# Delta-rule recurrence as two chains with banks and waits of their own, and the modulation chunks dealt out anew

## What is computed

```python
def gated_delta_chunk_scan(q, k, v, beta, log_a, s0):
    # a_mat = I + strict lower part of beta * (k k^T) * decay; w, u = a_mat^-1 applied to scaled k and v
    def step(state, inp):
        v_new = u_c - w_c @ state
        o = qd_c @ state + qk_c @ v_new
        state = gt_c * state + kd_c.T @ v_new
        return state, o

def run_bidirectional(...):      # one scan forward in time, one backward; their outputs are summed
    oc_f, sc_f = scan_fn(*ctx_fwd, s0);  ox_f, _ = scan_fn(*lat_fwd, sc_f)
    oc_b, sc_b = scan_fn(*flip(ctx_bwd), s0);  ox_b, _ = scan_fn(*flip(lat_bwd), sc_b)

sh1, sc1, g1, sh2, sc2, g2 = split(silu(c) @ w_mod + b_mod, 6)      # and the same for ada_w_2[0], ada_w_2[1]
```

## Time and profile before

| What | us |
|---|---|
| median of 3 runs | 3077.0 |
| lowest and highest | 3072.32, 3078.3 |
| the profiled execution, its own time | 3088.53 |
| its span, first to last instruction | 3086.6 |
| delta rule, half 0: first part, systems and transposes of the inverses, units of the inverses, recurrence, outputs | 396 to 493, 493 to 550, 550 to 646.9, 646.9 to 687.9, 687.9 to 702.6 |
| delta rule, half 1: systems, transposes of the inverses, units of the inverses, recurrence, outputs | 702.7 to 736.1, 736.1 to 751.1, 751.1 to 855.6, 855.6 to 922.9, 922.9 to 934.8 |

### The profile page before, as it was taken

The page is one execution under the profiler, slowest core; times in us unless marked ns, Lnnn a source line. Parts: engine busy times, 40 slices in busy tenths (PEclk is TensorE's granted clock), DMA queues, the critical chain, the costliest instruction groups (busy, mean ns, idle before and its releaser), DMA issues.

```text
span 3086.6 us, 36191 instructions
## 1 busy us (share of the span) xinstructions
PE 2854.6 (92%) x14765; PEld 2144.3 (69%) x14765; DVE 1205.1 (39%) x2187; ACT 579.2 (19%) x1109; POOL 432.9 (14%) x507
## 2 busy tenths in 40 slices
PE   6999978987978599999999989899999999999998
PEld 4677646975944378788878758578874486688843
DVE  2173642873425211111132485366750102576601
ACT  2102012121201211111132255122110111211200
POOL 2152403525411100000000000000110000000100
PEclk8999978998989699999999999899999999999999
DMA  9211340024271599899982200032222221322220
GB/s 368 75 41 42 110 176 27 3 110 164 83 286 43 192 339 333 322 333 331 323 286 83 69 1 1 1 98 93 82 76 75 92 68 41 99 86 82 89 75 27
DMA packets 202849, 403.15 MB, mean 131 GB/s; under 512 B 12850, under 2 KB 100450, under 8 KB 193506
## 3 DMA queue, kind: packets, MB, share of 16 engines
q1 hardware_dynamic: 195522, 375.15, 34.7%
q10 hardware_dynamic: 4896, 17.83, 1.4%
q0 software_dynamic: 2304, 8.39, 0.7%
HBM read 369.88 MB, written 31.46 MB: 130 GB/s over the span
## 4 chain that ended last, share of the span: by engine, by line
PE 84%; DVE 6%; DMA 3%; ACT 3%; issue 2%; POOL 1%; ACTq 0%; SPq 0%; POOLq 0%; DVEq 0%
PE ps L2704 17%; PE ps L1891 11%; PE ps L694 7%; PE ps L1909 5%; PE ps L1617 5%; PE ps L2718 5%; PE ps L2320 4%; PE ps L2733 4%; PE ps L2891 4%; PE ps L686 3%; PE ps L764 2%; PE ps L2462 2%; PE ps L385 2%; PE ps L2494 2%; DMA ring<-in_w_mod 2%
## 5 line engine op out<-in xcount | busy, mean ns | idle before, releaser
L1891 PEld LDWEIGHTS ps<-arena,ring 128*128 128x128 f32 x2944 | 334.2, 193 | 13.3 <-issue 10.5
L1891 PE MATMUL ps<-arena,ring 128*128 128x128 f32 x2944 | 334.5, 276 | 2.4 <-DMA ring<-in_w_gate 2.4
L2704 PE MATMUL ps<-arena 128*128 128x256 f32 x1056 | 235.3, 379 | 1.6 <-DVE arena L2801 1.6
L2704 PEld LDWEIGHTS ps<-arena 128*128 128x128 f32 x1056 | 200.5, 190 | 29.6 <-DVE arena L2801 2.4
L1617 PE MATMUL ps<-ring,hT 128*128 128x512 f32 x384 | 172.7, 606 | 4.2 <-DVE arena L2947 2.6
L694 PE MATMUL ps<-hT,ring 128*128 128x512 f32 x384 | 171.5, 601 | 2.5 <-ACT bet L1034 1.8
L2704 PE MATMUL ps<-hT,ring 128*128 128x256 f32 x704 | 164.9, 389 | 3.3 <-ACTq L200 3.3
L1909 PE MATMUL ps<-ring,arena 128*128 128x512 f32 x368 | 164.0, 598 | 1.8
L2704 PEld LDWEIGHTS ps<-hT,ring 128*128 128x128 f32 x704 | 137.5, 196 | 23.8 <-ACTq L200 4.1
L2718 PE MATMUL ps<-ring,arena 128*128 128x512 f32 x352 | 151.5, 592 | 1.3 <-issue 1.3
L2733 PE MATMUL ps<-ring,arena 128*128 128x512 f32 x352 | 151.7, 592 | 0.0
(11 more groups left out here) (480 smaller groups left out, 4535.8 us busy)
## 6 DMA issues: line engine op xcount, KB each, us to landing
ring<-in_ada_w SPq DMA_DIRECT2D x48, 1024.0 KB, 6.3
ring<-in_w_gate SPq DMA_DIRECT2D x46, 1024.0 KB, 6.6
ring<-in_w_up SPq DMA_DIRECT2D x46, 1024.0 KB, 5.7
ring<-in_w_down SPq DMA_DIRECT2D x46, 1024.0 KB, 5.4
ring<-in_ffn_w_up SPq DMA_DIRECT2D x44, 1024.0 KB, 5.0
ring<-in_w_mod SPq DMA_DIRECT2D x24, 1024.0 KB, 7.8
ring<-in_ffn_w_down SPq DMA_DIRECT2D x20, 1024.0 KB, 4.9
ring<-in_w_in SPq DMA_DIRECT2D x18, 1024.0 KB, 7.8
```

Source lines behind the costliest of these rows:

```text
L1891: last = pe.matmul(ps[:, t, f * P:(f + 1) * P], w[:, k, f * P:(f + 1) * P], xg[:, 4 * c + k, :], start=(c == 0 and k == 0 and f == 0), sto ...
L2704: last = pe.matmul(ps[:, u % 8, 0:HTOK], a[:, k, :], b[:, k, :], start=(k == 0), stop=(k == KD // 2 - 1))
```

## The change

The recurrence handles each direction d by itself. `ks`, `u` and `add` write banks `KSB`, `UB` and `AB`, two per kind, one a direction, and every hand-over (`ks_ps`, `z_ready`, `u_ps`, `u_ready`, `add_ps`, `dS_ready`) counts twice as fast, one step a direction, which `per_side` counts. The matmuls and DVE operations are the same in number and size, but for the dU of a direction, which was an instruction of its own already, and the first state copy, which is cut in two.

The chunks are dealt out anew. First part of half 0: 8 in one row before, now 4 ahead of the 32 transposes and 4 behind them. Systems: 0 and 12 before (halves 0 and 1), now 2 and 6. Inverses: 0 and 8, now 14 and 14, after every second unit from 8 to 34. Recurrence: 8 and 20, now 4 and 8. The last sums of the inverses come at their end. Since a group in bank 6 is now open during the systems of half 0, the projection units there all use bank 7 (`dn_bank`) and wait for the unit before to be copied. The token transposes of half 1 move to k = 2 and 3, four each, and DVE's normalisation steps start at k = 4 rather than 3. ACT's and SP's queues follow the same order; SP loads two chunks between the k and the v weights. POOL's group work is put at other points. The diff of ACT and SP, which repeats this, is left out.

```diff
-                if u >= 2:
+                if name == "dnp" and base and u >= QZ + 2:
+                    pe.wait_ge(s[name + "_out"], base + u)
+                elif u >= 2:
                     pe.wait_ge(s[name + "_out"], base + u - 1)
-                pe_unit(pe, W, name, units, u, 6 + u % 2)
+                pe_unit(pe, W, name, units, u, dn_bank(base and 1, u) if name == "dnp" else 6 + u % 2)
...
-        DN_MODS = [KD, [0] * NC, [0] * NC * LEVELS, [(0, 2), (2, 0), (0, 0), (0, 0), (1, 1), (1, 1)]], \
-            [0, [2] * NC, [int(u in range(10, 42, 4)) for u in range(NC * LEVELS)], [(0, 0)] + [(2, 2)] * 5]
-        DN_TOK = [(0, 0), (0, 2), (2, 1), (1, 2), (0, 0), (0, 0)]
+        def dn_bank(p, u):
+            return TURN_BANK if p and u >= QZ + 2 else 6 + u % 2
+
+        DN_FIRST = [4, 4]
+        DN_MODS = [[0, 2, 0, 0, 0, 0], [int(u in range(8, 36, 2)) for u in range(NC * LEVELS)], [(0, 0), (1, 0), (1, 0), (1, 0), (1, 0), (0, 0)]], \
+            [[1] * NC, [int(u in range(8, 36, 2)) for u in range(NC * LEVELS)], [(0, 0)] + [(1, 1)] * 3 + [(1, 0), (1, 0)]]
+        DN_TOK = [(0, 0), (0, 0), (2, 2), (2, 2), (0, 0), (0, 0)]
...
-            pe_mods(pe, W, DN_MODS[0][0], True)
+            pe_mods(pe, W, DN_FIRST[0], False)
             W.pay()
             pe.wait_ge(s["conv_done"], 1)
...
             last.then_inc(s["tok_ps"], 1)
+            pe_mods(pe, W, DN_FIRST[1], True)
             pe.wait_ge(s["mod_raw"], mods["pe"]["summed"])
             pe_units_between(pe, W, "dnp", DN_UNITS, DU, QZ, QZ + 2)
...
             if i == 0:
                 pe.wait_ge(s["conv_done"], 2)
+                pe.wait_ge(s["mod_raw"], mods["pe"]["summed"])
...
-                pe_mods(pe, W, DN_MODS[p][2][u], False)
+                pe_mods(pe, W, DN_MODS[p][1][u], u == NC * LEVELS - 1)
 
             pe.wait_ge(s["inv_out"], U0 + NC * LEVELS)
             toks, chans = iter(range(8)), iter(range(5))
             for k in range(NC):
                 if k:
-                    pe.wait_ge(s["dS_ready"], (NC - 1) * p + k)
                     for d in range(2):
+                        pe.wait_ge(s["dS_ready"], per_side(NC - 1, p, k - 1, d))
+                        c = ORDER[d][k]
+                        for h in range(2):
+                            last = pe.matmul(ps[:, KSB[d], h * P:(h + 1) * P], KT[:, c, h, :], dS[:, k - 1, 2 * d + h, :], start=True, stop=True)
+                        last.then_inc(s["ks_ps"], 1)
+                    pe_mods(pe, W, DN_MODS[p][2][k][0], False)
...
+                for d in range(2):
+                    if k:
+                        pe.wait_ge(s["z_ready"], per_side(NC - 1, p, k - 1, d))
+                    c = ORDER[d][k]
+                    for h in range(2):
+                        a = 2 * d + h
+                        last = pe.matmul(ps[:, UB[d], h * P:(h + 1) * P], XT[:, c, a, :], tv[:, c, h, :] if k == 0 else zb[:, a, :],
+                                         start=True, stop=True)
+                    last.then_inc(s["u_ps"], 1)
+                pe_mods(pe, W, DN_MODS[p][2][k][1], k == NC - 1 and p == 1)
+                if p == 0:
+                    for _ in range(DN_TOK[k][1]):
+                        pe_tok_group(pe, next(toks))
+                for d in range(2):
+                    pe.wait_ge(s["u_ready"], per_side(NC, p, k, d))
+                    if k < NC - 1:
+                        pe.wait_ge(s["kx_ready"], (NC - 1) * p + k + 1)
...
                         c = ORDER[d][k]
                         for h in range(2):
                             a = 2 * d + h
-                            last = pe.matmul(ps[:, 0, a * P:(a + 1) * P], KT[:, c, h, :], dS[:, k - 1, a, :], start=True, stop=True)
...
+        KSB, UB, AB = [0, 3], [1, 4], [2, 5]
+
+        def per_side(steps, p, k, d):
+
+            return 2 * (steps * p + k) + d + 1
...
-            if p:
-                pool_mods(g, ch, 6)
+            pool_mods(g, ch, 7 if p else 4)
...
-                    g.wait_ge(s["add_ps"], (NC - 1) * p + k - 1)
+                    g.wait_ge(s["add_ps"], 2 * ((NC - 1) * p + k - 1))
...
-                    v.wait_ge(s["ks_ps"], (NC - 1) * p + k)
                     for d in range(2):
+                        v.wait_ge(s["ks_ps"], per_side(NC - 1, p, k - 1, d))
                         c = ORDER[d][k]
                         for h in range(2):
-                            a = 2 * d + h
-                            last = v.scalar_tensor_tensor(out=zb[:, a, :], in0=ps[:, 0, a * P:(a + 1) * P],
+                            last = v.scalar_tensor_tensor(out=zb[:, 2 * d + h, :], in0=ps[:, KSB[d], h * P:(h + 1) * P],
                                                           scalar=nex[:, c, 4 * d + hs + h:4 * d + hs + h + 1],
                                                           in1=tv[:, c, h, :], op0=ALU.mult, op1=ALU.add)
-                    last.then_inc(s["z_ready"], 1)
-                    if p == 0 and k >= 3:
+                        last.then_inc(s["z_ready"], 1)
+                    if p == 0 and k >= 4:
                         next(norm, None)
...
-                v.wait_ge(s["u_ps"], NC * p + k + 1)
                 for d in range(2):
+                    v.wait_ge(s["u_ps"], per_side(NC, p, k, d))
                     c = ORDER[d][k]
-                    last = v.tensor_tensor(dU[:, c, 2 * d:2 * d + 2, :], ps[:, 1, 2 * d * P:2 * (d + 1) * P].rearrange("p (h x) -> p h x", h=2),
-                                           bc(bet[:, c, 4 * d + hs:4 * d + hs + 2], [P, 2, P], 2), ALU.mult)
-                last.then_inc(s["u_ready"], 1)
-                if p == 0 and k >= 3:
+                    v.tensor_tensor(dU[:, c, 2 * d:2 * d + 2, :], ps[:, UB[d], 0:2 * P].rearrange("p (h x) -> p h x", h=2),
+                                    bc(bet[:, c, 4 * d + hs:4 * d + hs + 2], [P, 2, P], 2), ALU.mult).then_inc(s["u_ready"], 1)
+                if p == 0 and k >= 4:
                     next(norm, None)
                 if k < NC - 1:
-                    v.wait_ge(s["add_ps"], (NC - 1) * p + k + 1)
-                    if k == 0:
-                        last = v.tensor_copy(dS[:, 0].rearrange("p a x -> p (a x)"), ps[:, 2, :])
-                    else:
-                        for d in range(2):
-                            c = ORDER[d][k]
+                    for d in range(2):
+                        v.wait_ge(s["add_ps"], per_side(NC - 1, p, k, d))
+                        c = ORDER[d][k]
+                        if k == 0:
+                            last = v.tensor_copy(dS[:, 0, 2 * d:2 * d + 2].rearrange("p a x -> p (a x)"), ps[:, AB[d], 0:2 * P])
+                        else:
+                            v.wait_ge(s["dS_ready"], per_side(NC - 1, p, k - 1, d))
                             for h in range(2):
                                 a = 2 * d + h
                                 last = v.scalar_tensor_tensor(out=dS[:, k, a, :], in0=dS[:, k - 1, a, :],
                                                               scalar=dex[:, 2, c, 4 * d + hs + h:4 * d + hs + h + 1],
-                                                              in1=ps[:, 2, a * P:(a + 1) * P], op0=ALU.mult, op1=ALU.add)
-                    last.then_inc(s["dS_ready"], 1)
-                    v.wait_ge(s["dS_ready"], (NC - 1) * p + k + 1)
-                    if p == 0 and k >= 3:
+                                                              in1=ps[:, AB[d], h * P:(h + 1) * P], op0=ALU.mult, op1=ALU.add)
+                        last.then_inc(s["dS_ready"], 1)
+                    if p == 0 and k >= 4:
                         next(norm, None)
```

55 lines of the change are left out of this document (18 added, 37 removed).

## The result

| | before | after |
|---|---|---|
| median, us | 3076.45 | 3041.58 |
| shortest and longest run, us | 3072.32 and 3078.30 (4 runs) | 3036.99 and 3047.55 (4 runs) |
| ratio to before, with its 95% interval | | 0.989, 0.9868 to 0.9911 |
| the profiled execution and its span, us | 3088.5, 3086.6 | 3047.55, 3045.7 |

What follows compares the result with a forecast made beforehand. PE was taken as the bound (84% of the chain), with gaps in a PE-DVE chain and chunks bunched faster than they load; -10 + 2 + 16 - 5 - 9 + 7.5 - 39 - 2.5 = -40 us gave 3037 us, range 3022 to 3059.

Steps and rivals of the forecast that it cites:

- part 3: Inverses of half 0: 14 chunks at 1.19 us plus sums, less 2 us for DVE's share: +16 us.
- part 6: Inverses of half 1: 6 more chunks at 1.19 us, and the last sums: +7.5 us.
- Part 1: First part of half 0: transposes fill the wait for chunks 5 to 8, k units start sooner: -10 us.
- cold k units: Rival: k units follow chunk waits, run at the lower clock, and lose the first part's 10 us: 3047 us, chance 0.09.
- Parts 2 and 5: Systems: half 0 takes two chunks, +2 us; half 1 has fewer chunks and POOL's chain sets it, -9 us.
- Part 4: Recurrence and outputs of half 0: 33 us against 39 up to the last dU, then +1: -5 us.
- Part 7: Recurrence of half 1: 8 chunks instead of 20 and shorter steps, 67.3 us to 28: -39 us.
- lock-step rival: Both recurrences: the directions don't slide past each other, a step stays near 7 us: 3052 us, chance 0.13.
- Loads still late: Rival: chunks at the end of half 1's recurrence wait for loads, four waits of 3 us: 3049 us, chance 0.07.
- More than counted: Rival: the lower bounds of four terms (first part, half 0's inverses, both recurrences) together, -51: 3026 us, chance 0.08.
- Slower: Rival: chunks in the inverses hold PE's queue for their loads, at 4 us a chunk +16: 3093 us, chance 0.03.
- No effect: Rival: a later stage, held by loads that start no sooner, takes the gain back: 3077 us, chance 0.03.

Runs made afterwards that it cites:

- the first part undone: Changed kernel with eight chunks again in one row ahead of the transposes of half 0's first part, the rest as changed: 3051.70 us, ratio 0.9923.
- the second set of runs: The changed kernel itself, unedited, timed once more beside the kernel before: 3039.46 us, ratio 0.9876.

## Why the prediction was right

**The bound.** PE was the chain, and the two wastes named (gaps in a chain of PE and DVE, chunks bunched faster than they load) are the two parts of the gain: each was removed alone, and each brought its own share (14.3 and 24.8 us).

**The price of a chunk, and parts 3 and 6.** A pair of units with one chunk takes 6.55 us in both halves of the changed kernel (here half 1, two starts), that is 2 x 2.68 + 1.19:

```profile
756.96 1.07 PE L385 MATMUL ps<-ring,gate 128*32 128x512 f32 x8
...
763.51 1.07 PE L385 MATMUL ps<-ring,gate 128*32 128x512 f32 x8
```

The price held to the hundredth, and no chunk in these rows waits for its load. What was mis-sized is around it. In part 3, 2 us were taken off because part of the stretch was thought to be DVE's. No chunk was covered in this way. PE's busy time grew by 112.72 - 94.98 = 17.7 us and the stretch by 17.3. PE does wait for DVE, but only in the last units, behind the last chunk: from the start of the last unit but four to `u`, half 0 takes 12.6 us before and 12.5 after, and half 1 takes 10.8 in the changed kernel. The row of the stretch had said as much, 95.0 busy of 96.9; the other reading compared half 0 with half 1, which differ in those last units, and also in how long their first products run at half clock (to the start of the next unit 6.56 us at a granted clock of 0.54 in half 0, and 5.08 at 0.71 in half 1).

In part 6 the last sums were counted at 0.4 us. They cost nothing: they lie in PE's wait for the last subtraction, and from the start of the last unit to `u` half 1 takes 3.68 us before and after. The 1.5 us beyond six chunks are two other things. First, the inverses began at half clock for longer, here first in the kernel before and then in the changed one:

```profile
751.12 3.45 PE L1145 MATMUL ps<-arena 128*128 128x128 f32 x16 [2.05 <-POOL arena L1334]
```

```profile
745.43 3.78 PE L1153 MATMUL ps<-arena 128*128 128x128 f32 x16 [2.04 <-POOL arena L1349]
```

The unit after these starts 5.08 us behind the first product in the one, at a granted clock of 0.71, and 6.07 in the other, at 0.58: 1.0 us. Second, in the unit behind a group's last chunk ACT copies the group (L418, 0.60 us) ahead of the unit's own copy, and PE waits for that: 0.41 us once a group, with one group more than before. The same two act in half 0, where the start at half clock was 0.9 us shorter than before (5.62 us at 0.63 instead of 6.56 at 0.54) and two groups end. Together parts 3 and 6 missed by 2.4 us, more than the 1.6 by which the sum did.

**Part 1** came out as worked (-10.5), the transposes back within 0.4 us of their forecast. One thing in it was not foreseen: the first k unit waits 1.82 us for its weights, and runs in 5.37 us instead of 3.62, at the lower clock for part of it. That the load has to wait until chunks 5 to 8 free their slots fits the order of SP's queue, but was not tried. The 1 us taken off for the clock and a start at 457 instead of 458 covered it. So the rival of cold k units came true in small: the first unit lost 1.75 us to the clock, where the rival had some 10 for the two. Here are the stretch of the first unit and that of the second, which took 7.03 us as before:

```profile
456.96:462.17 5.21, 5.21 (x17) 4.36 (x18) 0.00 (x0) 0.00 (x0) 0.00 (x0) 0.67 0.99 395
462.17:469.20 7.03, 7.02 (x17) 2.85 (x15) 0.00 (x0) 0.39 (x1) 0.00 (x0) 1.00 0.29 93
```

The granted clock was 1.00 from 449.6 to 455.2, in the chunks and the sums. When the first k unit began, behind its wait of 1.82 us for its weights, it was 0.50, and it stayed there until 460: that makes the 0.67 of the first row above, and the second has 1.00. In the kernel before, the transposes ahead of the k units began behind a wait of 3.88 us and ran at 0.50 until 467.3 and at 0.97 from there to 469.4, and the two k units at 1.00 from 469.4 to 479.9; with the first part undone these had 1.00, too, and took 3.62 and 7.03 us. So the k units did begin at the lower clock, as the rival had it, but the clock came back within the first of them, and that is why the price was 1.75 us and not 10.

**Parts 2 and 5** hit, +2.2 and -9.1, the first with some luck: three later traces with the same two chunks have 51.8 to 51.9 us there, which is +0.3. The new wait of the projection units costs nothing that shows. That POOL sets the pace in the systems of half 1 is borne out: POOL is busy 20.9 of 25.8 us there, PE waits for POOL for 6.9 us in all up to the first turn, and for no load.

**Part 4.** The steps with four token groups take 671.08 - 663.09 = 8.0 us where 7.6 was worked out, and the step with one chunk 4.7 instead of 4.5. Up to the last dU that makes 33.5 us, where 33 was forecast and 38.9 was the time before. The last sums, 2 us behind the last dU before, have left, and the outputs cost +1.6. So the parts are -5.3, -1.9 and +1.6, against -6 and +1 in the forecast: small misses that go against each other, -5.6 for -5.

**Part 7.** The mechanism is shown from both sides, with the chains and the chunks each undone. The lock-step rival (38 us for this stage) is what the kernel with one chain does, 36.0 us with steps of 6.90; the changed kernel took 28.4. The time of a step with two chunks was worked out at 5.2 us and measured 5.65, one with a single chunk at 4.5 and measured 882.70 - 877.91 = 4.79, from the chain of work. The chunk in the step is what was mis-sized. The steps of part 4 counted it at 1.0 us, its own length, where the same prediction had worked out a price of 1.19 from the earlier trace rows, with the change to other matmuls and back. In the chain u and a chunk take 865.27 - 863.18 = 2.09 us, that is 0.9 + 1.19. With this price the steps would have been 4.7 and 5.6; the remaining 0.1 us lies in ks, 1.23 us with its wait for the second direction's state. The 0.3 us a step that were added for "hand-overs that don't meet" took the place of both. So the stage came out at 28.4 for 28 partly by luck: the allowance had the right size for another reason. Loads still late is out: none stands in the chain of this stage.

**From the sum to the time.** The stages gave 38.4 us, the medians 34.9 and, in the second set of runs, 36.5. The forecast started from the traced execution, found 3048.5 for one like it, and 3047.55 was the profiled one: right within 1 us. It then took off the 11.5 us by which the execution before lay above its median. The changed kernel's own lay only 6 us above its median. The two traced executions, which both reach the first part late, differ by 41.0 us, against a forecast of 40. Of the two hypotheses for the rest of the medians' difference, a gain lost in a later stage or the scatter ahead of the first part, the traces speak for the second: from the end of the stages to the end of the program the two differ by 2151.7 against 2149.3 us, so nothing was given back there. Whether the chance of a late start differs between the kernels, three or four runs each can't tell.

**The other rivals.** More than counted (3026) is out by the stages, which gave 38.4 us and not 51. Slower (3093) is out: over the 20 chunks that moved into the inverses the change loses from 3.2 us a chunk on, and one costs 1.19. No effect is out by the stretch behind the stages, which is no longer than before.

## What to carry to other kernels

Here a chunk cost its whole 1.19 us where PE was full and next to nothing where it waited for POOL (12.8 and 13.3 us with six chunks in them, 12.9 and 13.5 without), so deal fillers by the busy time of each stretch, and look last at the short gaps between stages: 12 chunks moved into two gaps of 13 us were worth more than half of what the whole change had brought. With such fillers the granted clock also went up, from 0.66 to 1.00 in half 0, and behind a gap made longer elsewhere, 3.08 us instead of 1.72, it went down, from 1.00 to 0.50: look at the granted clock behind every wait that an edit changes. Where a chain and the loads behind its fillers both bind, undo each alone in turn; here the shorter chain was worth 5.7 us under late loads and 7.6 under punctual ones. Read a stretch's cover from its own row (length minus busy time), not from a comparison with a like stretch.

## What the runs showed of the hardware

**POOL beside DVE.** The masks of the inverses are the same instruction throughout. First the changed kernel, inverses of half 0, then the same in half 1 (line, count, busy us and mean ns of one, idle before):

```profile
L1349 POOL TENSOR_TENSOR arena<-arena,levm 128x256 f32<-128x256 f32 x70 | 59.8, 875 | 48.8 <-PE ps L1153 48.8
```

```profile
L1349 POOL TENSOR_TENSOR arena<-arena,levm 128x256 f32<-128x256 f32 x70 | 49.4, 727 | 59.0 <-PE ps L1153 59.0
```

In half 0 DVE runs the convolution beside them, and a mask takes 875 ns on average (780 in the kernel before), in half 1 727 (728 before). The convolution's instructions took longer together with the masks: those of 441 columns 853 ns before and 926 after. No run here takes the convolution away. Why the masks became slower with the chunks in the stretch, when DVE's instructions are the same 132, was not tried. It cost nothing, since POOL has 49 us of idle time there.

**The clock of identical code.** The same code, from 40 to 60 us, ran at a granted clock of 0.73 to 0.74 in three traces and at 0.91 to 0.97 in the other eight, at 362 to 377 GB/s of DMA in all. What sets it was not tried.
